# Wide value projections, halved low parts, moved modulation groups and early dilated scores in a two-block transformer kernel

## The chip, the cores and the metric

The kernel runs on one core of a Trainium2 chip, in one launch. The metric is the device time of an execution in microseconds. The engines are TensorE (PE; its weight loads are the row PEld), VectorE (DVE), ScalarE (ACT), GpSimd (POOL) and SyncE (SP), whose queue issues nearly all loads.

## What is computed

256 tokens of width 1024 pass through a first block of two layers, and a second block that is modulated by a conditioning vector `c_2`. The change lies in the second block and in the last attention of the first. In the reference:

```python
mod = jax.nn.silu(c) @ w_ada[l] + b_ada[l]
sh1, sc1, g1, sh2, sc2, g2 = jnp.split(mod, 6, axis=-1)
h = modulate(rms_norm(x, norm1_g[l]), sh1, sc1)
x = x + g1[:, None, :] * token_mixer(h, w_in[l], rel_bias, ...)
h = modulate(rms_norm(x, norm2_g[l]), sh2, sc2)
x = x + g2[:, None, :] * squared_relu_mlp(h, w_ff1[l], w_ff2[l])
```

`token_mixer` projects h with `w_in` into retention queries, keys and values (`rq`, `rk`, `rv`: 4 heads, values 512 wide each), three groups of dilated attention (`aq`, `ak`, `av`: 512 columns each), and gates (`rg`, `ga`, `gb`), runs the retention and the dilated attention, projects both branches, and merges them.

## The kernel before

**Groups and units.** All projections are an ordered list, `PLAN`. A group is one fill of one of three PSUM banks; a unit is one load of at most 128 x 2048 fp32 weights (1 MB). A unit name with "a" or "b" is half of a group's weights. `WEIGHTS`, `LOADS` and the slot tables are worked out from the list: a unit's raw slot is the one whose last unit is oldest, and SP loads it once that unit's group has been read.

**Two precisions.** In the first block the matmuls are plain fp32 (line 571; in the profile each counts as two matmuls). From `rq0` on, a weight unit is split: ScalarE copies its high part to fp32r (`w_hi`, line 1050, called by `passing`), GpSimd subtracts to get the low part (`w_lo`, line 521, one instruction for a unit), and TensorE does three fp32r matmuls for each product: high x high, high x low, low x high (lines 596 to 598, with the weights stationary and 256 tokens moving; lines 628 to 630 for values, with 128 tokens stationary and 256 value columns moving).

**ScalarE's order.** ScalarE works in program order. At each group it comes to, it first calls `passing(name)`:

```python
if max(old, LOADED_AFTER[v]) >= GROUP_AT[name]:
    break
...
act.wait_ge(raw_in[RAW_AT[n]], raw_target(n))
nc.scalar.activation(hi_slots[HI_AT[m]][:, 0:kt * w], raw_slots[RAW_AT[n]][:, 0:kt * w], ACT.Copy)
```

It splits the next units in order, as long as their high slot's last reader and the groups that their load (and all loads ahead of it) waited for come before `name`. `LOADED_AFTER` is the index of the last such group. For rq0 and rq1 it is `ad11`, for rq2 `wo1_1`.

**Modulation.** `mod` is made of 12 groups `ad0` to `ad11`, each of two 1 MB units, 16 matmuls in the profile (line 810), a transpose and a copy on VectorE (lines 1505 and 1507), and is gathered by `modA` and `modB`. They are placed by hand between other work: `FILL_CD` lists, for the 16 units of attention C and D, what is done before and after the transposes of a unit ("/" parts the two). C has 12 units, D 4.

**Attention.** For a unit: scores (TensorE), maximum (VectorE), exponential (ScalarE, line 1116), normalisation (VectorE, line 1484), transposes (TensorE, line 702), copies (ScalarE, line 1134), product with the values. Between C/D and rq0 lies `output(1, ...)`: four groups `wo1_0` to `wo1_3`, residual, squares (ScalarE, line 1098), their sums in pairs (VectorE, line 1683) and over partitions (TensorE, line 644), then the norm of stream x2, whose last steps make `parts`, the split h (line 1383). `output(2, ...)` does the same for x3.

**Block 2's order on TensorE.** rq, rk (8 groups), rv (8 groups of 256 columns), four retention heads with the groups of `RET_FILL` between their steps, the last values av2_0 and av2_1, dilated attention with the gates as fill (`FILL_A`), the branch products `wr0`, `wa0` to `wa3`, `wr1` to `wr3`, the output product `wo2`, then `f1` and `f2`.

## Time and profile before

| | |
|---|---|
| median of 3 runs | 1031.07 us (1030.75 to 1032.62) |
| the profiled execution | 1030.22 us, span 1028.4 us |
| granted TensorE clock, mean | 0.976 |
| busy: PE, PEld, DVE, ACT, POOL | 93%, 85%, 35%, 40%, 43% of the span |
| chain that ended last | PE 84%, DVE 10%, ACT 3%, issue 1%, DMA 1% |

Times in the rows count from the start of the span. A matmul's row gives its latency; back-to-back matmuls overlap, so the distance between starts is what one costs. A number in brackets at a row's end is the idle time of that engine before it, and what ended it. L571 is line 571 of the kernel before.

### The profile page before, as it was taken

To read this page: it belongs to the slowest core of one execution; us is meant where nothing else is said; L and a number is where in the kernel's file an instruction comes from. 1 tells how busy PE (TensorE), PEld (TensorE's weight loads), DVE (VectorE), ACT (ScalarE), POOL (GpSimd) and SP (SyncE) were. 2 spreads that over 40 slices of the span, in tenths; PEclk is the share of its full clock that TensorE was granted. 3 is DMA by queue.
4 is the path that set the end of the run, shared out by engine and by line. 5 is a ranking of instruction groups with operands and counts; after the bars stand their busy time and mean duration, and the time that the engine had idled before them with its cause. 6 is when DMAs were issued, how large, how long until landed. Compare 5 with 4: busy or idle time off the path is not lost.

```text
span 1028.4 us, 15967 instructions
## 1 busy us (share of the span) xinstructions
PE 957.8 (93%) x6896; PEld 874.2 (85%) x6896; DVE 363.5 (35%) x734; ACT 408.1 (40%) x588; POOL 446.0 (43%) x101
## 2 busy tenths in 40 slices
PE   4999889999898798999999998999999979999996
PEld 4887677788676377999999998999999979999996
DVE  4677521320556626640111113222115643341002
ACT  3111541013576423234343444667533545553330
POOL 0000000000000031787766665766787767886780
PEclk9999899999899999999999998999999989999998
DMA  9632245858524363565534443444544625453531
GB/s 353 257 123 82 83 175 205 329 176 316 196 83 164 124 246 126 175 242 183 185 131 158 158 150 111 160 161 152 177 164 164 238 95 200 168 199 130 204 121 41
DMA packets 27470, 177.51 MB, mean 173 GB/s; under 512 B 2904, under 2 KB 5476, under 8 KB 6920
## 3 DMA queue, kind: packets, MB, share of 16 engines
q1 hardware_dynamic: 25960, 174.28, 46.9%
q10 hardware_dynamic: 1440, 2.20, 0.7%
q8 instruction: 55, 0.90, 0.3%
q14 instruction: 15, 0.12, 0.0%
HBM read 174.88 MB, written 3.43 MB: 173 GB/s over the span
## 4 chain that ended last, share of the span: by engine, by line
PE 84%; DVE 10%; ACT 3%; issue 1%; DMA 1%; POOL 0%; DVEq 0%; ACTq 0%
PE proj L571 18%; PE proj L596 14%; PE proj L597 14%; PE proj L598 14%; PE proj L628 3%; PE proj L630 3%; PE proj L629 3%; PE proj L780 3%; PE proj L617 2%; PE transposed L702 2%; PE proj L810 2%; PE mixed L731 1%; PE scores L690 1%; DVE parts L1561 1%; PE scores L677 1%
## 5 line engine op out<-in xcount | busy, mean ns | idle before, releaser
L521 POOL TENSOR_TENSOR w_lo<-raw,w_hi 128x2048 fp32r<-128x2048 f32 x71 | 329.0, 4639 | 269.7 <-ACT w_hi L1050 269.6
L596 PE MATMUL proj<-parts,w_hi 128*128 128x256 f32 x768 | 222.2, 289 | 6.5 <-DVE parts L1383 4.2
L597 PE MATMUL proj<-parts,w_lo 128*128 128x256 f32 x800 | 227.5, 284 | 0.0
L598 PE MATMUL proj<-parts,w_hi 128*128 128x256 f32 x768 | 218.3, 284 | 0.0
L1050 ACT ACTIVATE w_hi<-raw 128x2048 fp32r<-128x2048 f32 x71 | 135.5, 1909 | 99.4 <-PE proj L598 63.8
L596 PEld LDWEIGHTS proj<-parts,w_hi 128*128 128x128 f32 x768 | 148.1, 193 | 8.1 <-issue 5.2
L597 PEld LDWEIGHTS proj<-parts,w_lo 128*128 128x128 f32 x800 | 154.2, 193 | 0.8 <-issue 0.7
L598 PEld LDWEIGHTS proj<-parts,w_hi 128*128 128x128 f32 x768 | 148.0, 193 | 0.0
L525 POOL MEMSET probT<- 128x512 f32 x1 | 0.5, 525 | 247.8 <-PE proj L897 247.8
L571 PE MATMUL proj<-h,raw 128*128 128x256 f32 x320 | 76.5, 403 | 3.0 <-DVE h L1391 3.0
L571 PEld LDWEIGHTS proj<-h,raw 128*128 128x128 f32 x320 | 64.7, 204 | 14.2 <-issue 4.5
L628 PE MATMUL proj<-w_hi,parts 128*128 128x256 f32 x224 | 64.0, 286 | 0.0
L629 PE MATMUL proj<-w_lo,parts 128*128 128x256 f32 x224 | 63.4, 283 | 0.0
L630 PE MATMUL proj<-w_hi,parts 128*128 128x256 f32 x224 | 63.4, 283 | 0.0
L571 PE MATMUL proj<-h,arena 128*128 128x256 f32 x256 | 56.8, 381 | 1.1 <-DVE h L1391 1.1
L571 PEld LDWEIGHTS proj<-h,arena 128*128 128x128 f32 x256 | 48.2, 190 | 10.6 <-issue 3.6
L1098 ACT ACTIVATE wide<-xT 128x512 f32<-128x512 f32 (+1 forms) x24 | 13.2, 556 | 104.8 <-DVE xT L1790 64.0
L571 PE MATMUL proj<-arena 128*128 128x256 f32 x224 | 49.4, 380 | 0.0
L571 PEld LDWEIGHTS proj<-arena 128*128 128x128 f32 x224 | 42.4, 190 | 6.0 <-issue 0.3
L596 PE MATMUL proj<-hid_hi,w_hi 128*128 128x256 f32 x160 | 45.1, 282 | 0.0
L597 PE MATMUL proj<-hid_hi,w_lo 128*128 128x256 f32 x160 | 44.7, 279 | 0.0
L598 PE MATMUL proj<-hid_lo,w_hi 128*128 128x256 f32 x160 | 44.6, 279 | 0.0
(273 smaller groups left out, 1940.5 us busy)
## 6 DMA issues: line engine op xcount, KB each, us to landing
raw<-in_weights SPq DMA_DIRECT2D x113, 1024.0 KB, 4.9
arena<-in_weights SPq DMA_DIRECT2D x36, 1024.0 KB, 5.0
probT<-in_weights SPq DMA_DIRECT2D x8, 1024.0 KB, 5.7
dil_lines<-dil_line SPq DMA_DIRECT2D x1, 2304.0 KB, 12.1
dil_bias<-dil_lines SPq DMA_DIRECT2D x1, 1536.0 KB, 9.6
xT<-in_x SPq DMA_DIRECT2D x2, 512.0 KB, 5.6
arena<-in_alibi SPq DMA_DIRECT2D x1, 1024.0 KB, 20.6
arena<-in_swa SPq DMA_DIRECT2D x1, 1024.0 KB, 7.3
```

Of the source, the lines that this page charges most:

```text
L521: nc.gpsimd.tensor_tensor(lo_slots[RAW_AT[n]][:, 0:kt * w], raw_slots[RAW_AT[n]][:, 0:kt * w], hi_slots[HI_AT[m]][:, 0:kt * w].bitcast(F32 ...
L571: last = nc.tensor.matmul(b[:, S * j:S * j + S], w[:, k, P * j:P * j + P], src[:, k, :], start=first, stop=done and (k == ks[-1] if not wa ...
L596: nc.tensor.matmul(dst, whi, h, start=first, stop=False)
L597: nc.tensor.matmul(dst, wlo, h, start=False, stop=False)
L598: last = nc.tensor.matmul(dst, whi, lo[:, k, :], start=False, stop=stop)
L617: last = nc.tensor.matmul(b[:, S * t:S * t + n], h32[:, k, P * t:P * t + P], w[:, k, 0:n], start=k == 0, stop=k == KD - 1)
L628: nc.tensor.matmul(dst, parts[:, 0, k, at], whi[:, k, c:c + n], start=k == 0, stop=False)
L629: nc.tensor.matmul(dst, parts[:, 0, k, at], wlo[:, k, c:c + n], start=False, stop=False)
L630: last = nc.tensor.matmul(dst, parts[:, 1, k, at], whi[:, k, c:c + n], start=False, stop=k == KD - 1)
L702: last = nc.tensor.transpose(pt[0:w, P * i:P * i + P], prob(u)[:, i, P * r:P * r + w], ident[:])
L780: last = nc.tensor.matmul(b[:, 2 * c:2 * c + S], w[:, k, c:c + P], h32[:, k, :], start=k == 0, stop=k == KD - 1)
L1050: nc.scalar.activation(hi_slots[HI_AT[m]][:, 0:kt * w], raw_slots[RAW_AT[n]][:, 0:kt * w], ACT.Copy) \
```

## The change

- The 14 value groups of 256 columns become seven of 512 columns, each of two units of 512 rows x 512 columns and two PSUM banks, one for each 128 tokens (`token_rows` takes the place of `tokens`). The unit "a" is used for both banks before "b".
- GpSimd makes each low part in two instructions, and TensorE waits for the first half at a unit's start and for the second at its middle (`second_half`).
- `ad8`, `ad9` and `ad11` leave `FILL_CD`, and `ad7` moves by one unit. `ad8` and `ad9` are done before and after the last sum of x2, `ad10` and `ad11` before and after the last sum of x3, with a gathering `modC` of their own after `f1_2`. Their loads move: ad8 and ad9 stand ahead of rq2, ad10 and ad11 ahead of f1_2; from ad9 on they have slots of their own in memory free by then.
- The scores of the first unit of dilated attention are issued ahead of the last value group, those of the second between its halves.
- The slot tables and `LOADED_AFTER` follow from the list. For rq0 and rq1 it is now `ad6`, for rq2 and rq3 `wo1_2`, for f1_2 `wo2_0` as before.

```diff
-RET_FILL = [f"a{n}{g}_{i}" for g in range(AG) for n in "qk" for i in range(2)] + \
-    [f"av{g}_{i}" for g in range(AG) for i in range(2)]
+RET_FILL = [x for g in range(AG) for x in ([f"aq{g}_{i}" for i in range(2)], [f"ak{g}_{i}" for i in range(2)])] + \
+    [[f"av{g}"] for g in range(AG)]
...
-    "/ zd1.1", "/ E:zd1 ad6", "/ modA", "/ ad7", "/ ad8", "/ ad9", "/", "/ ad11")]
+    "/ zd1.1", "/ E:zd1 ad6", "/ modA", "/", "/ ad7", "/", "/", "/")]
...
-    out += own([f"wo1_{i}" for i in range(4)]) + [(n, parts_of(n)) for n in ("ad10",)]
+    out += own([f"wo1_{i}" for i in range(4)]) + [(n, parts_of(n)) for n in ("ad8", "ad9")]
     out += own(["rq0"]) + [("modB", [])]
-    out += own([f"rq{i}" for i in range(1, 4)] + [f"rk{i}" for i in range(4)] + [f"rv{i}" for i in range(8)])
+    rows = lambda n: [(n, [f"{n}a"]), (f"{n}:0", [f"{n}b"]), (f"{n}:1", [f"{n}b"])]
+    dilated = lambda names: rows(*names) if names[0][1] == "v" else own(names)
+    out += own([f"rq{i}" for i in range(1, 4)] + [f"rk{i}" for i in range(4)]) + [x for i in range(RH) for x in rows(f"rv{i}")]
     for h in range(RH):
-        out += own(RET_FILL[4 * h:4 * h + 4]) + [(f"rt{h}_0", []), (f"rt{h}_1", [])]
-    out += own(RET_FILL[16:]) + own(GATED)
+        out += dilated(RET_FILL[2 * h]) + dilated(RET_FILL[2 * h + 1]) + [(f"rt{h}_0", []), (f"rt{h}_1", [])]
+    out += dilated(RET_FILL[8]) + own(GATED)
     out += [(n, [f"{n}a", f"{n}b"] if n[1] == "r" else [f"wa{int(n[2]) // 2}"]) for n in BRANCHES]
-    out += own([f"wo2_{i}" for i in range(4)] + [f"f1_{i}" for i in range(16)])
+    out += own([f"wo2_{i}" for i in range(4)]) + [(n, parts_of(n)) for n in ("ad10", "ad11")]
+    out += own([f"f1_{i}" for i in range(3)]) + [("modC", [])] + own([f"f1_{i}" for i in range(3, 16)])
...
-SPLIT = WEIGHTS[WEIGHT_AT["rq0"]:]
+BANKED = [g for g in GROUPS if f"{g}:1" not in GROUP_AT]
+BANK_AT = {n: i for i, n in enumerate(BANKED)}
+SPLIT = [u for u in WEIGHTS[WEIGHT_AT["rq0"]:] if u[:2] != "ad"]
...
-LOADS = [u for u in WEIGHTS if u[:4] != "ad10"]
-for _n, _u in enumerate(("ad10a", "ad10b")):
-    LOADS.insert(LOADS.index("rq2") + _n, _u)
+LOADS = [u for u in WEIGHTS if u[:3] not in ("ad8", "ad9", "ad1") or u[:4] in ("ad1a", "ad1b")]
+for _before, _us in (("rq2", ("ad8a", "ad8b", "ad9a", "ad9b")), ("f1_2", ("ad10a", "ad10b", "ad11a", "ad11b"))):
+    for _n, _u in enumerate(_us):
+        LOADS.insert(LOADS.index(_before), _u)
...
+        elif u in ALONE:
+            most = max(most, GROUP_AT["wr3" if u[2] == "1" else "ad7"])
...
+                elif u[:3] == "ad9":
+                    sp.wait_ge(po_free, STEPS_TO["d"])
+                elif u[:3] == "ad1":
+                    sp.wait_ge(proj_ready, GROUP_AT["wr3"] + 1)
...
-                nc.gpsimd.tensor_tensor(lo_slots[RAW_AT[n]][:, 0:kt * w], raw_slots[RAW_AT[n]][:, 0:kt * w],
-                                        hi_slots[HI_AT[m]][:, 0:kt * w].bitcast(F32), ALU.subtract).then_inc(lo_ready, 1)
+                for half in range(2):
+                    at = slice(kt * w // 2 * half, kt * w // 2 * (half + 1))
+                    nc.gpsimd.tensor_tensor(lo_slots[RAW_AT[n]][:, at], raw_slots[RAW_AT[n]][:, at],
+                                            hi_slots[HI_AT[m]][:, at].bitcast(F32), ALU.subtract).then_inc(lo_ready, 1)
...
+            def second_half(u, k):
+                if k == unit_shape(u)[0] // 2 and state["lo"] < SPLIT_AT[u]:
+                    pe.wait_ge(lo_ready, 2 * SPLIT_AT[u] + 2)
+                    state["lo"] = SPLIT_AT[u]
...
-            def tokens(name, c, n):
-                b = begin(name)
-                whi, wlo = weight(UNITS_OF[name][0])
-                for t in range(TT):
-                    for k in range(KD):
-                        dst, at = b[:, S * t:S * t + n], slice(P * t, P * t + P)
-                        nc.tensor.matmul(dst, parts[:, 0, k, at], whi[:, k, c:c + n], start=k == 0, stop=False)
-                        nc.tensor.matmul(dst, parts[:, 0, k, at], wlo[:, k, c:c + n], start=False, stop=False)
-                        last = nc.tensor.matmul(dst, parts[:, 1, k, at], whi[:, k, c:c + n], start=False, stop=k == KD - 1)
-                end(last)
+            def token_rows(name, middle=None):
+                banks = [None] * TT
+                for half in "ab":
+                    u = f"{name}{half}"
+                    whi, wlo = weight(u)
+                    for t in range(TT):
+                        if half == "a":
+                            banks[t] = begin(f"{name}:{t}")[:]
+                        for k in range(4):
+                            at, kk = slice(P * t, P * t + P), 4 * (half == "b") + k
+                            nc.tensor.matmul(banks[t], parts[:, 0, kk, at], whi[:, k, :], start=kk == 0, stop=False)
+                            second_half(u, k)
+                            nc.tensor.matmul(banks[t], parts[:, 0, kk, at], wlo[:, k, :], start=False, stop=False)
+                            last = nc.tensor.matmul(banks[t], parts[:, 1, kk, at], whi[:, k, :], start=False, stop=kk == KD - 1)
+                        if half == "b":
+                            end(last)
+                    if half == "a":
+                        last.then_inc(proj_ready, 1)
+                        if middle is not None:
+                            middle()
...
-            output(1, "x2", product, lambda i: ada("ad10") if i == 0 else None)
+            output(1, "x2", product, lambda i: ada(f"ad{8 + i}"))
             project("rq0", fresh=2)
-            pe.wait_ge(sem("ada_cols"), ADA_GROUPS)
-            mod_columns("modB", ADA_ONE, ADA)
+            pe.wait_ge(sem("ada_cols"), ADA_GROUPS - 2)
+            mod_columns("modB", fold, ada_cols, ADA_ONE, ADA_TWO)
             for name in [f"rq{i}" for i in range(1, 4)] + [f"rk{i}" for i in range(4)]:
                 project(name)
-            for i in range(8):
-                tokens(f"rv{i}", 0, 256)
-            def dilated_fill(name):
-                if name[1] == "v":
-                    tokens(name, 0, 256)
-                else:
-                    project(name)
+            for i in range(RH):
+                token_rows(f"rv{i}")
...
-            for name in RET_FILL[16:]:
-                dilated_fill(name)
-            pe.wait_ge(*evacuated("av2_1"))
-            attention(PART["a"], FILL_A)
+            for n in "qk":
+                for i in range(2):
+                    pe.wait_ge(*evacuated(f"a{n}2_{i}"))
+            scores(PART["a"][0])
+            token_rows("av2", lambda: scores(PART["a"][1]))
+            for t in range(TT):
+                pe.wait_ge(*evacuated(f"av2:{t}"))
+            attention(PART["a"], FILL_A, 2)
...
+            pe.wait_ge(sem("late_silu_ready"), 1)
+            output(2, "x3", merged_product, lambda i: ada(f"ad{10 + i}", late_silu))
             for i in range(16):
                 project(f"f1_{i}", fresh=3 if i == 0 else None)
+                if i == 2:
+                    pe.wait_ge(sem("late_fold_in"), 16)
+                    pe.wait_ge(sem("ada_cols"), ADA_GROUPS)
+                    mod_columns("modC", late_fold, late_cols, 0, ADA - ADA_TWO)
...
-            for name in RET_FILL[16:]:
-                dilated_out(name)
-            attention(PART["a"], FILL_A)
+            passing("av2")
+            exps(PART["a"][0])
+            dilated_out(RET_FILL[8])
+            attention(PART["a"], FILL_A, 1)
...
-            ada_out("ad10")
-            mod_out("modB", ADA_ONE, ADA)
+            ada_out("ad8")
+            ada_out("ad9")
+            mod_out("modB", ADA_ONE, ADA_TWO)
+            V.tensor_copy(late_silu, silu_c).then_inc(sem("late_silu_ready"), 1)
...
+            for name in ("ad10", "ad11"):
+                ada_out(name, late_flip, late_cols, 10)
             for i in range(16):
+                if i == 3:
+                    mod_out("modC", ADA_TWO, ADA)
```

## Rows read from the trace of the kernel before

**Rows 1.** The page, busy time in us, share of the span, instructions.
```profile
PE 957.8 (93%) x6896; PEld 874.2 (85%) x6896; DVE 363.5 (35%) x734; ACT 408.1 (40%) x588; POOL 446.0 (43%) x101
```
**Rows 2.** Timeline of ScalarE in the value projections: start us, us.
```profile
485.78 0.60 ACT L1066 ACTIVATE arena<-proj 128x512 f32<-128x512 f32 x1 [3.37 <-PE proj L630]
...
491.54 0.60 ACT L1066 ACTIVATE arena<-proj 128x512 f32<-128x512 f32 x1 [3.37 <-PE proj L630]
```
**Rows 3.** The chain, plain fp32 of 256 and of 512 columns.
```profile
380.00 6.91 PE proj L571 x32
...
510.93 1.72 PE mixed L984 x4
```
**Rows 4.** The page's costliest groups: GpSimd's low parts, one of three value lines.
```profile
L521 POOL TENSOR_TENSOR w_lo<-raw,w_hi 128x2048 fp32r<-128x2048 f32 x71 | 329.0, 4639 | 269.7 <-ACT w_hi L1050 269.6
...
L628 PE MATMUL proj<-w_hi,parts 128*128 128x256 f32 x224 | 64.0, 286 | 0.0
```
**Rows 5.** The chain in attention C/D (L810 is group ad6).
```profile
323.15 1.85 PE proj L810 x16
...
329.59 1.28 ACT L1116
...
332.68 1.11 PE transposed L702 x4
...
339.44 0.64 DVE dil_bias L1505
...
340.10 0.18 DVE arena L1507
```
**Rows 6.** Timeline of SP: loads of rq0 and rq1; the one issued behind wo1_2.
```profile
360.92 0.90 SPq L478 DMA_DIRECT2D raw<-in_weights  x2
...
386.94 0.33 SPq L478 DMA_DIRECT2D arena<-in_weights  x1
```
**Rows 7.** Timeline of ScalarE: splits of rq0 and rq1, x2's last squares.
```profile
367.99 1.91 ACT L1050 ACTIVATE w_hi<-raw 128x2048 fp32r<-128x2048 f32 x1 [4.18 <-DMA raw<-in_weights]
370.40 1.92 ACT L1050 ACTIVATE w_hi<-raw 128x2048 fp32r<-128x2048 f32 x1 [0.50 <-DMA raw<-in_weights]
...
395.01 0.63 ACT L1098 ACTIVATE wide<-xT 128x512 f32<-128x512 f32 x1 [6.68 <-DVE xT L1689]
```
**Rows 8.** Timeline of TensorE: a sum of x2, and behind both norms of block 2.
```profile
379.30 0.70 PE L644 MATMUL sums<-wide,cols 128*128 128x256 f32 x2 [1.85 <-DVE wide L1683]
...
401.74 0.55 PE L596 MATMUL proj<-parts,w_hi 128*128 128x256 f32 x1 [4.15 <-DVE parts L1383]
...
832.66 0.55 PE L596 MATMUL proj<-parts,w_hi_b 128*128 128x256 f32 x1 [4.62 <-DVE parts L1383]
```
**Rows 9.** The chain, a load of 1 MB from issue to landing.
```profile
750.22 4.90 DMA raw<-in_weights
```
**Rows 10.** Timeline of VectorE: three subtractions beside GpSimd's low parts.
```profile
786.96 15.12 DVE L1561 TENSOR_TENSOR parts<-arena,parts 128x512 fp32r<-128x512 f32 x3
```
**Rows 11.** Timeline of TensorE at the start of the dilated attention.
```profile
620.66 0.94 PE L677 MATMUL scores<-arena 128*128 128x128 f32 x6 [0.69 <-ACT arena L1066]
622.63 2.38 PE L677 MATMUL scores<-arena 128*128 128x256 f32 x6 [1.03 <-DVE stat L1426]
626.22 1.65 PE L677 MATMUL scores<-arena 128*128 128x128 f32 x6 [1.21 <-DVE stat L1426]
...
628.10 0.41 PE L598 MATMUL proj<-parts,w_hi 128*128 128x256 f32 x1
628.31 0.41 PE L596 MATMUL proj<-parts,w_hi 128*128 128x256 f32 x1
```
**Rows 12.** Timeline of TensorE ahead of wr3 and inside wo2_0.
```profile
786.64 0.35 PE L596 MATMUL proj<-yret_hi,w_hi_a 128*128 128x256 f32 x1 [2.03 <-POOL w_lo_a L521]
...
804.93 0.38 PE L596 MATMUL proj<-parts,w_hi 128*128 128x256 f32 x1 [1.00 <-DVE parts L1561]
```
**Rows 13.** Busy us in a window (PE, PEld, DVE, ACT, POOL), granted clock, DMA, GB/s.
```profile
786.60:792.00 5.40, 5.36 (x32) 5.39 (x33) 5.40 (x3) 2.55 (x2) 5.26 (x2) 0.68 0.84 350
```

More of the change, by code:

```diff
@@ L139 @@
 EARLY = [NRAW + 2 + i for i in range(3)]
+ALONE = {u: NRAW + 5 + i for i, u in enumerate(("ad9a", "ad9b", "ad10a", "ad10b", "ad11a", "ad11b"))}
 def raw_slots_of(n, u):
+    if u in ALONE:
+        return [ALONE[u]]
     if u in SPLIT_AT:
@@ L531, in _ @@
         def _(pe):
-            state = dict(filled=0, norm=0, head=0, stream=0)
+            state = dict(filled=0, norm=0, head=0, stream=0, lo=-1)
             def begin(name):
-                m = GROUP_AT[name]
+                m = BANK_AT[name]
                 assert state["filled"] <= m < state["filled"] + NPP, name
@@ L782, in chunk, with attention @@
                     end(last)
-            def attention(units, fill):
-                scores(units[0])
-                scores(units[1])
+            def attention(units, fill, begun=0):
+                for u in units[begun:2]:
+                    scores(u)
                 for i, u in enumerate(units):
@@ L986, in _ @@
                     last.then_inc(sem("ret_out"), 1)
-                for i in range(2, 4):
-                    dilated_fill(RET_FILL[4 * h + i])
+                dilated_fill(RET_FILL[2 * h + 1])
                 pe.wait_ge(sem("ret_normed"), 2 * h + 2)
@@ L1027, in _ @@
             stream_sums("xf", 3)
-            assert state["filled"] == len(GROUPS) and state["norm"] == len(NORMS)
+            assert state["filled"] == len(BANKED) and state["norm"] == len(NORMS)
         @block.scalar
@@ L1171, in between, with attention @@
                     copy_out(name, fl((gaT if name[1] == "a" else gbT)[:, 2 * i:2 * i + 2]), fn=ACT.Sigmoid)
-            def attention(units, fill):
-                exps(units[0])
+            def attention(units, fill, begun=0):
+                for u in units[begun:1]:
+                    exps(u)
                 for i, u in enumerate(units):
@@ L1292, in _, with dilated_out @@
                 passing(name)
[L1293 to L1303 removed]
+            for i in range(RH):
+                passing(f"rv{i}")
+                for t in range(TT):
+                    copy_out(f"rv{i}:{t}", rv[:, t, RDV * i:RDV * i + RDV])
+            def dilated_out(names):
+                for name in names:
+                    g, i = int(name[2]), int(name[-1])
+                    if name[1] == "v":
+                        passing(name)
+                        for t in range(TT):
+                            copy_out(f"{name}:{t}", av[:, g, t, :])
+                    else:
+                        copy_out(name, (aqT if name[1] == "q" else akT)[:, g, 512 * i:512 * i + 512],
+                                 scale=P ** -0.5 if name[1] == "q" else 1.0)
             for h in range(RH):
[L1306 to L1308 removed]
+                dilated_out(RET_FILL[2 * h])
+                passing(RET_FILL[2 * h + 1][0])
                 for t in range(TT):
@@ L1311, in _ @@
                     nc.scalar.activation(bn[:, t, 8:9], bn[:, t, 8:9], ACT.Sqrt).then_inc(sem("ret_sqrt"), 1)
-                for i in range(2, 4):
-                    dilated_out(RET_FILL[4 * h + i])
+                dilated_out(RET_FILL[2 * h + 1])
                 for half in range(2):
@@ L1500, in mixed_out, with ada_out @@
                 V.tensor_tensor(y, cut(po[:, 0:S], P), y, ALU.mult).then_inc(po_free, 1)
-            def ada_out(name):
-                g = int(name[2:])
-                V.transpose(ada_flip, ready(name)[:]).then_inc(free_of(name), 1)
+            def ada_out(name, flip=ada_flip, table=ada_cols, first=0):
+                g = int(name[2:]) - first
+                V.transpose(flip, ready(name)[:]).then_inc(free_of(name), 1)
                 dve.wait_ge(*evacuated(name))
-                V.tensor_copy(ada_cols[:, 16 * g:16 * g + 16], cut(ada_flip, HROW)[:, :, 0]).then_inc(sem("ada_cols"), 1)
+                V.tensor_copy(table[:, 16 * g:16 * g + 16], cut(flip, HROW)[:, :, 0]).then_inc(sem("ada_cols"), 1)
                 state["cols"] = state.get("cols", 0) + 1
```

70 lines of the change are left out of this document (36 added, 34 removed).

## The prediction

> **What bounds the kernel now.** I read the page first: TensorE is busy 93% of the span [rows 1], and the chain of work that ended last runs through it for 84%. So work taken off TensorE counts, and work of another engine counts only where TensorE waits for it. Next the timelines of the stages that the diff touches, and the chain of waits, to find those places. They are few: the attention of branches C and D (up to 363 us), where the chain passes from engine to engine [rows 5]; the two norms of block 2, where TensorE stands still for 4.15 and 4.62 us [rows 8]; the start of the dilated attention [rows 11]; and two waits around the last branch product [rows 12]. Everything from rq0 to av2 is back to back.
>
> **Value projections (removes 672 fp32r matmuls of 256 columns, adds 336 of 512).** One group of 48 old matmuls takes 5.76 us, the distance of the copies behind two groups [rows 2]: 120 ns each. There are 14 such groups, 224 matmuls in each of three lines [rows 4]. No fp32r matmul of 512 columns is in the trace. If the time went with the columns it would be 240 ns: gain nothing. The other end is the plain pass, in which 256 columns take 6.91/32 = 216 ns and 512 take 1.72/4 = 430 ns [rows 3], 214 for 256 more: almost no fixed part. At full clock 256 columns of fp32r need half a plain pass, 108 ns, and take 120, so 12 ns is something else: hidden when the matmul is longer (216 ns for 512), or paid once per matmul (228 ns). At half clock the pitch is 0.21 us [rows 11], exactly twice 107, with no 12 ns on top, which speaks for hiding. I take 220: 336 x (240 - 220) = -6.7 us, bounds 0 and -8.1.
> The Trainium skill (TensorE: Matmul & The Clock Gate, "Back-to-back issue gap") gives columns/2.4 + 2.5 ns: 216 ns for 512, by which the gain would be 8.1 us. By that rule 256 columns would take 109 ns, and the trace shows 120, so it is not followed to the end here.
>
> **First dilated scores around the last values.** Before, TensorE ends av2_1 at 619.97, waits 0.69 for the copy, does the scores of three units with waits of 1.03 and 1.21 between them, and starts rg0 at about 627.5, at half clock [rows 11]: 7.6 us. After, unit 0's scores lie before av2, unit 1's between its halves, where VectorE has 5 us to take the banks. What stays is three units at full clock, 6 x 0.108 + 6 x 0.216 + 6 x 0.108 = 2.6 us, and one copy wait, 0.7: 3.3 us. That is -4.3. The twelve matmuls of rg0 at 213 instead of 120 ns cost 1.1, and go too: -5.4 (bounds -3 and -6).
>
> **Low parts in halves.** A low part is 4.64 us of GpSimd [rows 4]. Two halves are 2.3 us each if time goes with size; a shorter one is not in the trace. A fixed cost matters only above 0.27 us a half, since TensorE needs 24 x 216 = 5.2 us for a unit. TensorE can start on the first half. Where weights are ready early this gains nothing, which is nearly everywhere. It gains before wr3: TensorE waits 2.03 us, until 786.6, for a low part that must have begun at about 782.0 [rows 4, 12]; its first half is done at 784.3, before TensorE is free at 784.6. Behind that wait the granted clock is 0.68 for 5.4 us [rows 13], that is some 3.4 us at half rate, 1.7 us lost. Together -3.7. But VectorE's subtractions stand behind GpSimd: three of them took 15.12 us [rows 10], one behind each GpSimd instruction. With halves each waits at most 2.3, yet the last subtraction before wo2_0 still comes two halves, a scale and a copy after wr3, so the wait of 1.00 [rows 12] grows by about 1.2. Net -2.5 (bounds -3.7 and -1).
> The Trainium skill (SBUF — State Buffer, "Who interferes with whom") says a VectorE instruction with two SBUF inputs and a GpSimd one that reads SBUF exclude each other for a whole instruction. The trace agrees [rows 10]. It also means that two such VectorE instructions in a row gain nothing from halves: the second waits for the second half. I count none for the rotary.
>
> **Modulation groups moved.** A group is 1.85 us of TensorE, and 0.64 of VectorE for the transpose and 0.18 for the copy [rows 5]. Three leave C/D. TensorE waits there for VectorE, so what counts is two times 0.85 of VectorE on the chain (at 339.44, and once more at 351.87) and most of the 1.85 of ad11: -3.3. The groups that arrive later lie in the two norm waits [rows 8]; ad10 of block 2's second norm stands in front of the last sum and costs some 0.5 us.
>
> **What moves with them: loads, and ScalarE's splits.** This is the part that speaks against the change. ScalarE works in order, and its routine passing() splits every unit whose slots are free by the group it stands at, waiting for the load. Removing ad8, ad9 and ad11 from the list frees rq0's and rq1's raw slots early: they count as loaded after ad6, not ad11. So ScalarE does them at modA, ahead of the exponentials of unit 11. Their loads are third and fourth of four that SP issues when ad6 has been read, at 325.0 (1.85 us from 323.15) [rows 5]. A lone megabyte lands 4.90 us after its issue [rows 9]; in a line they land 2.4 us apart (splits at 367.99 and 370.40 for loads of 360.92) [rows 6, 7]. So rq0 lands at 325.0 + 4.9 + 2 x 2.4 = 334.7, rq1 at 337.1; with 1.91 us for a split, ScalarE is free at 339.0. Before, it went on at 329.59, and from there to TensorE's transposes at 332.68 the chain runs through it [rows 5]. Cost +9.5 us, all of it on the chain. Behind it GpSimd's two low parts run into VectorE's normalisation of unit 11: +0.8 (0 to 2.3).
> For the same reason the splits of rq0 and rq1 are gone from the output stage, and with them the low part that held VectorE's sum of squares and TensorE for 1.85 us [rows 8]: -1.85.
> rq2 moves too. Before, it was loaded ahead of ad10b; now SP issues it fourth behind ad8b, ad9a and ad9b, when wo1_2 has been read at 386.9 [rows 6]. It lands at 386.9 + 4.9 + 3 x 2.4 = 399.0. ScalarE must split it at wo1_3, before the last squares, which began at 395.01 [rows 7]. So the squares end at 399.0 + 1.9 + 0.6 = 401.5, TensorE's four sums at 402.6 instead of 397.6 (401.74 less the 4.15 us) [rows 8]. +5.0, and +0.5 as rq2's low part holds the norm's first product: +5.5 (bounds 4 and 7).
> In the second norm f1_2 is behind four modulation loads in the same way, but about 22 us after wr3 it still lands almost in time: +0.7 with ad10.
>
> **The clock.** C/D has less TensorE work and one pause of 10 us; the first norm's pause is longer too; in the second, ad11 shortens a pause of 4.62 us. A stretch at half clock of 3.4 us costs 1.7. I take +1.0 (bounds -2 and +6).
>
> **The sum:** -6.7 -5.4 -2.5 -3.3 -1.85 +9.5 +0.8 +5.5 +0.7 +1.0 = -2.3 us. I leave half a microsecond for waits of VectorE behind the second half of a low part (two ada_out in a row ahead of modB among them): -1.8. The profiled execution took 1030.22 us (span 1028.4 and 1.8 around it), so 1028.4; the median of the runs is 0.85 above it: 1029.3 us.
>
> **Rivals.** (1) *ScalarE's waits are cheap*: the loads land earlier than in my line, or the exponentials behind them had slack. For it: the chain near 330 changes engines every microsecond. Against it: both splits are fixed by the order on ScalarE, and 3.8 us of them is pure work. Without both waits (-9.5 - 0.8 - 5.5): 1013.5 us; with half of them 1021. (2) *The wide matmuls gain nothing*: the fp32r pass is bound by 0.469 ns a column. For it: 120 ns for 256 columns and no wide fp32r row. Against it: the half-clock pitch [rows 11]. It gives +6.7, 1036 us, and decides (slower than before) from a pitch above 228 ns on, all else as summed. (3) *The clock*: C/D and the first output product run at half rate, which adds 5 us: 1034.5. For it: the removed groups were what filled TensorE there, and a pause of 2.03 us was enough to lower the clock before wr3 [rows 12, 13]. Against it: behind the pauses of 1.85 and 1.00 us it stayed up [rows 8, 12].
>
> **Chances.** Forecast 0.50 (own range 1024 to 1034), rival 1 0.14, rival 2 0.16, rival 3 0.20. A measurement of this kernel can tell about 0.2%, 2.1 us. The forecast gives 0.30 faster, 0.15 same, 0.05 slower; rival 1 is all faster; rival 2 gives 0.13 slower, 0.03 same; rival 3 0.12 slower, 0.05 same, 0.03 faster. Together 0.47, 0.23, 0.30. The range is 1017 to 1037: below it lies rival 1 in full, above it rivals 2 and 3 together.
>
> **What the profile after would show.** The wide matmuls' pitch between two value copies (220 ns or 240); a ScalarE idle of 5 us ended by a load at about 330, with TensorE still until about 342; a split of rq2 ended by a load at about 399 less the shifts before, with the last squares behind it; the dilated scores split around av2 with one wait; no wait before wr3. It is wrong above all if ScalarE does not stand still at modA, or if the exponentials of unit 11 were not what the chain needed.

## The result, and the profile after

The changed kernel takes 1037.19 us in the median of 11 runs (1036.38 to 1040.58), the kernel before 1031.09 in 11 runs beside it (1029.12 to 1036.76). The ratio is 1.0054, 95% interval 1.0035 to 1.0072: slower by 5.6 us, where 1029.3 was forecast; it lies just above the range. The profiled execution took 1039.65 us, its span is 1037.9, 9.5 more than before.

The page of the kernel after: the span, busy time by engine, the chain by engine, and GpSimd's low parts.

```profile
span 1037.9 us, 15403 instructions
...
PE 958.2 (92%) x6562; PEld 855.9 (82%) x6562; DVE 394.5 (38%) x739; ACT 409.2 (39%) x588; POOL 467.6 (45%) x197
...
PE 83%; DVE 9%; DMA 4%; ACT 2%; issue 1%; SPq 0%; DVEq 0%; ACTq 0%
...
L542 POOL TENSOR_TENSOR w_lo<-raw,w_hi 128x1024 fp32r<-128x1024 f32 x142 | 341.3, 2426 | 271.6 <-ACT w_hi L1096 271.6
```

What has grown is DMA, from 1% to 4% of the chain: TensorE ends up waiting for loads, through ScalarE. To see where, I set the same instruction of both traces side by side. The shift is its start after less its start before; the last columns are what each stretch added and what the prediction's terms say for it.

| up to | before | after | shift | added | forecast |
|---|---|---|---|---|---|
| transposes ahead of modA | 327.23 | 328.66 | 1.4 | +1.4 | 0 |
| transposes behind the splits (C/D) | 332.68 | 344.48 | 11.8 | +10.4 | +9.5 |
| last product of D | 362.34 | 374.81 | 12.5 | +0.7 | -1.5 |
| third x2 sum | 394.08 | 406.82 | 12.7 | +0.3 | -1.85 |
| rq0 | 401.74 | 421.95 | 20.2 | +7.5 | +5.5 |
| scores of retention head 1 (holds rv) | 524.87 | 541.52 | 16.65 | -3.6 | -3.8 |
| products of head 3 (holds av0) | 593.27 | 609.32 | 16.05 | -0.6 | -1.0 |
| wr0 (holds av1, av2, the early scores) | 738.95 | 748.47 | 9.5 | -6.5 | -7.3 |
| wo2_0 | 804.93 | 811.52 | 6.6 | -2.9 | -2.5 |
| third x3 sum | 818.94 | 824.99 | 6.05 | -0.5 | 0 |
| f1_0 | 832.66 | 842.63 | 10.0 | +3.9 | +0.7 |
| last f2 sums | 1018.37 | 1027.84 | 9.5 | -0.5 | 0 |

(A value group's share of -6.7 is one in seven, 0.96: four in the line of head 1, whose measured -3.6 holds 1.1 us of another cause, rq0 at full clock. The row of D holds three terms: -3.3 for the groups removed, +1.0 for the clock, +0.8 for the low parts behind the splits. The half microsecond held back for waits of VectorE is in no row.) The change wins nearly what it should from rq1 to wo2_0 and loses it at three places. Here they are in the timelines of the kernel after (start, duration, engine, line, operation, tiles, count, and in brackets the idle time before it with what ended it).

C/D, first ScalarE, then TensorE:

```profile
330.41 0.59 ACT L1180 ACTIVATE probT<-transposed 128x512 f32<-128x512 f32 x1
337.00 1.91 ACT L1096 ACTIVATE w_hi<-raw 128x2048 fp32r<-128x2048 f32 x1 [6.00 <-DMA raw<-in_weights]
339.45 1.91 ACT L1096 ACTIVATE w_hi<-raw 128x2048 fp32r<-128x2048 f32 x1 [0.54 <-DMA raw<-in_weights]
341.38 1.28 ACT L1162 ACT_TABLE_LOAD   x1
...
331.61 0.33 PE L856 MATMUL proj<-arena 128*128 128x64 f32 x2
344.48 1.11 PE L741 MATMUL transposed<-cols,wide 128*128 128x128 f32 x4 [12.53 <-ACT probT L1180]
...
348.57 1.03 PE L741 MATMUL transposed<-cols,prob 128*15 128x128 f32 x4 [0.97 <-DVE prob L1535]
...
354.24 3.64 PE L849 MATMUL proj<-raw,arena 128*32 128x512 f32 x16
```

ScalarE stands 6.54 us for the loads of rq0 and rq1 and works 3.82 us on them, together 10.36: the 10.4 that the stretch added. Behind it ad7 takes 3.64 us instead of the 1.92 of a group at full clock: half clock. The low parts of rq0 and rq1 run on GpSimd from 338.99 to 348.24, and VectorE beside them:

```profile
343.97 1.99 DVE L1524 TENSOR_SCALAR stat<-stat 128x4 f32<-128x4 f32 x1 [10.49 <-ACT prob L1162]
...
346.21 2.05 DVE L1533 TENSOR_TENSOR stat<-stat,arena 128x4 f32<-128x4 f32 x1
```

With the splits out of the way (late splits, below) these two take 0.17 and 0.16 us. TensorE waits 0.97 us for their result at 348.57: that is the +0.8 of the forecast.

The x2 output, with SP's issues, ScalarE and TensorE:

```profile
399.68 0.80 SPq L496 DMA_DIRECT2D arena<-in_weights  x2
...
401.00 1.41 SPq L496 DMA_DIRECT2D raw<-in_weights  x2
...
413.25 1.91 ACT L1096 ACTIVATE w_hi<-raw 128x2048 fp32r<-128x2048 f32 x1 [12.21 <-DMA raw<-in_weights]
415.06 0.61 ACT L1144 ACTIVATE wide<-xT 128x512 f32<-128x512 f32 x1
...
407.35 1.92 PE L849 MATMUL proj<-arena 128*32 128x512 f32 x16
415.73 2.07 PE L683 MATMUL sums<-wide,cols 128*128 128x256 f32 x4 [6.46 <-ACT wide L1144]
417.73 3.41 PE L849 MATMUL proj<-arena 128*32 128x512 f32 x16
421.95 0.35 PE L623 MATMUL proj<-parts,w_hi 128*128 128x256 f32 x1 [0.81 <-DVE parts L1434]
```

The first of the line's loads is issued at 399.68, rq2 as the fourth at 401.00. ScalarE's split of rq2 starts at 413.25, 12.25 us behind its own issue and 13.6 behind the line's first; ScalarE has stood for it 12.21 us with the last squares behind it.

The x3 output, in the same order and with VectorE's fold:

```profile
806.29 2.28 SPq L496 DMA_DIRECT2D arena<-in_weights  x4
813.24 18.44 SPq L496 DMA_DIRECT2D raw<-in_weights  x4
...
828.52 1.92 ACT L1096 ACTIVATE w_hi<-raw 128x2048 fp32r<-128x2048 f32 x1 [7.97 <-DMA raw<-in_weights]
830.34 0.61 ACT L1144 ACTIVATE wide<-xT 128x512 f32<-128x512 f32 x1
...
830.99 2.18 DVE L1734 TENSOR_TENSOR wide<-wide 128x256 f32<-128x256 f32 x1 [4.93 <-ACT wide L1144]
...
833.22 0.70 PE L683 MATMUL sums<-wide,cols 128*128 128x256 f32 x2 [1.90 <-DVE wide L1734]
833.85 3.56 PE L849 MATMUL proj<-arena,sq 128*32 128x512 f32 x16
842.63 0.36 PE L623 MATMUL proj<-parts,w_hi_b 128*128 128x256 f32 x1 [2.30 <-DVE parts L1434]
```

The same once more, and not foreseen: f1_2's load, issued at 813.24 behind seven megabytes (wo2_3, f1_0, f1_1 and the four of ad10 and ad11, from 804.97 on), lands for a split at 828.52. Squares, fold and sum are late in turn, and ad10 runs at half clock.

The wide matmuls, by ScalarE's copies of the token half 0 of two value units:

```profile
478.57 0.60 ACT L1108 ACTIVATE arena<-proj 128x512 f32<-128x512 f32 x1 [0.80 <-PE proj L664]
...
489.45 0.60 ACT L1108 ACTIVATE arena<-proj 128x512 f32<-128x512 f32 x1 [0.80 <-PE proj L664]
```

10.88 us for 48 matmuls: 227 ns each, against 2 x 120 before [rows 2].

### The profile page after: what moved, and what is told of

Its sections match the earlier page's. It is cut to its first block, busy times and chain, and to the rows that moved or that the text cites. A ratio compares the mean times of both kernels' runs of the same rounds, so it can differ in the third digit from the quotient of the medians.

```text
span 1037.9 us, 15403 instructions
## 1 busy us (share of the span) xinstructions
PE 958.2 (92%) x6562; PEld 855.9 (82%) x6562; DVE 394.5 (38%) x739; ACT 409.2 (39%) x588; POOL 467.6 (45%) x197
## 4 chain that ended last, share of the span: by engine, by line
PE 83%; DVE 9%; DMA 4%; ACT 2%; issue 1%; SPq 0%; DVEq 0%; ACTq 0%
PE proj L598 17%; PE proj L623 14%; PE proj L626 14%; PE proj L625 14%; DMA raw<-in_weights 4%; PE proj L819 3%; PE proj L664 2%; PE proj L663 2%; PE proj L661 2%; PE proj L645 2%; PE proj L849 2%; PE transposed L741 2%; PE mixed L770 1%; PE scores L729 1%; DVE rstd L1438 1%
## 5 line engine op out<-in xcount | busy, mean ns | idle before, releaser
L542 POOL TENSOR_TENSOR w_lo<-raw,w_hi 128x1024 fp32r<-128x1024 f32 x142 | 341.3, 2426 | 271.6 <-ACT w_hi L1096 271.6
L598 PEld LDWEIGHTS proj<-h,raw 128*128 128x128 f32 x320 | 63.3, 199 | 13.7 <-issue 4.5
L1108 ACT ACTIVATE arena<-proj 128x512 f32<-128x512 f32 x40 | 23.9, 598 | 78.0 <-PE proj L626 48.8
L661 PE MATMUL proj<-w_hi,parts 128*128 128x512 f32 x112 | 44.4, 396 | 0.0
L1860 DVE TENSOR_TENSOR hid_lo<-tmp,hid_hi 128x512 fp32r<-128x512 f32 x16 | 43.7, 2732 | 0.6
## 6 DMA issues: line engine op xcount, KB each, us to landing
dil_lines<-dil_line SPq DMA_DIRECT2D x1, 2304.0 KB, 12.1
```

The lines of the kernel that those rows point to most:

```text
L542: nc.gpsimd.tensor_tensor(lo_slots[RAW_AT[n]][:, at], raw_slots[RAW_AT[n]][:, at], hi_slots[HI_AT[m]][:, at].bitcast(F32), ALU.subtract).t ...
L598: last = nc.tensor.matmul(b[:, S * j:S * j + S], w[:, k, P * j:P * j + P], src[:, k, :], start=first, stop=done and (k == ks[-1] if not wa ...
L661: nc.tensor.matmul(banks[t], parts[:, 0, kk, at], whi[:, k, :], start=kk == 0, stop=False)
L1108: nc.scalar.activation(dst, b[:], fn, scale=scale).then_inc(free_of(name), 1)
L1860: V.tensor_tensor(two(hid_lo, i), r, two(hid_hi, i).bitcast(F32), ALU.subtract).then_inc(sem("hid_ready"), 1)
```

## Experiments

Times are turned into microseconds as ratio x 1032; "less than after" compares the ratio of a kernel with 1.0054. The times of one kernel spread: those of the kernel before, all visits together, from 1026.9 to 1038.1 us. Some of it is the granted clock in the attention of D, which differs between two executions of one kernel ("Two profiles of one kernel"). So small differences are checked in traces.

### Mending the orders: three places

**Late splits.** In ScalarE's passing():

```diff
+                    if v in ("rq0", "rq1"):
+                        old = GROUP_AT["ad7"]
```

> The kernel after, but ScalarE splits rq0 and rq1 only from wo1_0 on, when the attention of branches C and D is over; the loads and everything else stay. Main theory (ScalarE standing still 6.0 us for rq0's load and working 3.8 us on the two splits is what moved TensorE's transposes from 332.68 to 344.48 us, and the half clock behind it is the consequence of that pause): TensorE's pause is gone, the clock in D is full, and the time falls by 8 to 11 us, to about 1028 us; up to 2 us of it are given back since GpSimd's low parts of rq0 or rq1 meet VectorE's squares of the x2 sum again. Rival (the pauses in D and its half clock come from the three modulation groups that no longer fill TensorE there): the clock stays at half in D and only the 4 us of pure waiting go: 1033 us or more. If ScalarE had slack there: no change, 1037 us.

**rq2 first.** In the list of loads:

```diff
-for _before, _us in (("rq2", ("ad8a", "ad8b", "ad9a", "ad9b")), ...
+for _before, _us in (("rq3", ("ad8a", "ad8b", "ad9a", "ad9b")), ...
```

> The kernel after, but rq2 is loaded ahead of ad8a, ad8b, ad9a and ad9b (right behind wo1_3), so that ScalarE needs not wait for it before the last squares of the x2 sum. Main theory (TensorE's 6.46 us at the last x2 sum are the wait of ScalarE for rq2, fourth in its line of loads): the wait falls to about 1 us, the sums and ad9 run at full clock, and the time falls by 5 to 8 us, to about 1031 us. Rival (the wait goes to the next in the line: ad9, now loaded last, is what TensorE waits for behind the sums): 0 to 2 us, 1036 us.

**Both.**

> Both edits at once: rq0 and rq1 split from wo1_0 on, and rq2 loaded ahead of ad8 and ad9. Main theory: the two losses are independent and add up: 13 to 17 us less than the kernel after, about 1022 us, well under the kernel before. Rival (they share a cause, or the early load only moves the low parts of GpSimd in front of VectorE's squares): not more than the better of the two alone, 1028 us.

Late splits: ratio 0.9935 (0.9912 to 0.9957), 12.3 us less than after. rq2 first: 1.0002 (0.9985 to 1.0020), 5.4 less. Both: 0.9883 (0.9862 to 0.9904), 17.7 less, which is the sum of the two. rq2 first lies in its expected range of 5 to 8 us; late splits, expected at 8 to 11, and both, expected at 13 to 17, won a little more than their ranges. The main theory holds for all three, and the kernel with both is well under the one before. In the trace of the kernel with late splits, TensorE's pause and its successors read so:

```profile
334.35 0.66 PE L741 MATMUL transposed<-cols,wide 128*128 128x128 f32 x4 [2.17 <-ACT probT L1182]
...
364.12 1.97 PE L770 MATMUL mixed<-probT,arena 128*64 128x128 f32 x16 [0.69 <-ACT probT L1182]
...
405.36 2.07 PE L683 MATMUL sums<-wide,cols 128*128 128x256 f32 x4 [6.43 <-ACT wide L1146]
```

12.53 us of waiting have become 2.17, while the 6.43 at the x2 sum stand as they were: they are the other place's. One expectation failed: the clock in D is not full again. The lines give, from the transposes behind the splits to the last product of D, the length, TensorE's busy time and, third from the end, the granted clock, for the kernel before (the profile of the prediction), after, late splits, and the kernel before profiled again:

```profile
332.68:362.34 29.66, 21.55 (x192) 11.57 (x192) 19.18 (x50) 12.15 (x45) 0.00 (x0) 0.94 0.32 112
```
```profile
344.48:374.81 30.33, 20.12 (x145) 12.24 (x145) 20.15 (x46) 12.29 (x45) 3.76 (x2) 0.73 0.00 1
```
```profile
334.35:364.12 29.77, 20.55 (x144) 12.48 (x144) 16.52 (x44) 12.39 (x45) 0.00 (x0) 0.64 0.13 56
```
```profile
332.89:367.92 35.03, 26.56 (x193) 13.48 (x193) 19.17 (x50) 12.16 (x45) 0.00 (x0) 0.76 0.28 98
```

0.73 with the pause ahead, 0.64 without it, over the same instructions. So the half clock in D does not need the pause. The rival's clock came true, but not its time. Its cause, the three groups gone, is not shown: with the groups in place the second profile of the kernel before has 0.76.

**Three orders.** The x3 output mended too: f1_2 loaded ahead of ad10, f1_3 ahead of ad11.

```diff
-... ("f1_2", ("ad10a", "ad10b", "ad11a", "ad11b"))):
+... ("f1_3", ("ad10a", "ad10b")), ("f1_4", ("ad11a", "ad11b"))):
```

> The kernel with both orders mended (1020.3 us), and in the x3 output f1_2 loaded ahead of ad10a and ad10b, f1_3 ahead of ad11a and ad11b. There, ScalarE stood 8.11 us for f1_2's load with the squares of the third sum behind its split, and TensorE stood 2.03 us and then ran at half clock. Main theory (a third case of a weight load placed behind modulation loads): that idle time of ScalarE and the 2.03 us go, ad10 takes 1.9 us instead of 3.4, and the time falls by 3 to 4 us, to about 1017 us. Rival (TensorE now waits for ad11's load, or the gain lies within the norm's own wait): 0 to 1 us.

Ratio 0.9838 (0.9812 to 0.9864), 4.6 us less than with two orders (0.9862 to 0.9904; the intervals just touch). TensorE there:

```profile
813.13 0.59 PE L683 MATMUL sums<-wide,cols 128*128 128x256 f32 x2
813.65 1.92 PE L849 MATMUL proj<-arena,sq 128*32 128x512 f32 x16
815.50 1.13 PE L683 MATMUL sums<-wide,cols 128*128 128x256 f32 x4
816.56 1.92 PE L849 MATMUL proj<-arena,sq 128*32 128x512 f32 x16
821.27 0.35 PE L623 MATMUL proj<-parts,w_hi_b 128*128 128x256 f32 x1 [2.78 <-DVE parts L1436]
```

No wait before the third sum, and both groups at full clock inside what was the norm's pause: this is what the move of the groups was meant to look like.

**Held splits.** The other cure: no load is moved, only ScalarE's order, at all three places.

```diff
+                    held = {"rq0": "ad7", "rq1": "ad7", "rq2": "ad9", "f1_2": "ad11", "f1_3": "ad11"}.get(v)
+                    if held is not None:
+                        old = max(old, GROUP_AT[held])
```

> The kernel after with every load where it is, and only ScalarE's order changed at all three places: rq0 and rq1 are split from wo1_0 on, rq2 from rq0 on, f1_2 and f1_3 from f1_0 on, behind the squares that they held. If the harm is ScalarE waiting in order, and not the place of the loads as such: as good as the three mended orders of loads, about 1016 us. Rival (the low parts then fall on VectorE's products of the norms, which TensorE waits for): 1019 to 1024 us.

Ratio 0.9833 (0.9816 to 0.9851), 1015.43 us: as good as the three orders and the lowest median here, 1.7% under the kernel before. So what did the harm is ScalarE waiting in order ahead of work that the chain needs; the late loads alone cost nothing that can be measured here. The rival's collision is there and small: TensorE waits 0.90 us at modB and 1.45 at rq2 for VectorE.

**Early loads.** The loads of rq0 and rq1 put ahead of wo1_0, as soon as their slots are read.

```diff
+for _u in ("rq0", "rq1"):
+    LOADS.remove(_u)
+    LOADS.insert(LOADS.index("wo1_0"), _u)
 LOADS.remove("wo1_3")
-LOADS.insert(LOADS.index("rq1") + 1, "wo1_3")
+LOADS.insert(LOADS.index("wo1_2") + 1, "wo1_3")
```

> The kernel after, but rq0 and rq1 are loaded ahead of wo1_0 (as soon as their slots come free, behind zc1 and zd0), so that ScalarE splits them earlier in C and never waits for their data. It tells the two parts of the loss apart. Main theory (the waiting for the loads, some 6.5 us, is the larger part, and two splits of 1.91 us with GpSimd's low parts beside VectorE the smaller): 5 to 8 us less than the kernel after, about 1031 us. If the work alone is the trouble (ScalarE's chain is that tight, and a low part holds VectorE wherever it falls): 0 to 3 us less, 1035 us.

A miss: 1.0049 (1.0032 to 1.0065), nothing gained. ScalarE in C, then TensorE:

```profile
300.73 1.91 ACT L1099 ACTIVATE w_hi<-raw 128x2048 fp32r<-128x2048 f32 x1 [3.31 <-DMA raw<-in_weights]
...
320.06 1.91 ACT L1099 ACTIVATE w_hi<-raw 128x2048 fp32r<-128x2048 f32 x1 [1.95 <-DMA raw<-in_weights]
```
```profile
308.16 1.11 PE L744 MATMUL transposed<-cols,prob 128*128 128x128 f32 x4 [4.85 <-DVE prob L1538]
...
327.03 0.61 PE L744 MATMUL transposed<-cols,prob 128*15 128x128 f32 x4 [2.91 <-DVE prob L1538]
...
343.45 0.66 PE L744 MATMUL transposed<-cols,wide 128*128 128x128 f32 x4 [2.17 <-ACT probT L1183]
```

The splits moved forward with the loads, because passing() takes each unit as soon as the group that read its slot is behind: the load is issued at that same moment. ScalarE still waits 5.26 us, and TensorE's pauses stand in C instead (in the trace of late splits it does not wait there). I had thought the waiting would be gone; it went from 6.54 to 5.26 only, so this run doesn't tell waiting from work. That the loss is both (6.54 + 3.82) rests on the trace of after alone.

### The parts one by one

**Groups back.** All of the change but the move of the modulation groups: FILL_CD, the list of loads, the x2 and x3 outputs and modB as before.

> The kernel after with the modulation groups where they were before (ad8, ad9 and ad11 in C and D, ad10 at the x2 output, none in the x3 output), all else as after: wide value projections, low parts in halves, early dilated scores. Main theory (only the move of the groups loses time; the after trace shows 227 ns for a wide matmul, so 4.5 us won, 5.5 for the early scores, 2.9 before wo2_0): 1031.1 - 12.9 = 1018 us. Rival (halves of low parts cost VectorE and GpSimd time elsewhere, or the wide matmuls win nothing): 1024 to 1031 us.

Ratio 0.9864 (0.9833 to 0.9896), 14.0 us under the kernel before. The three other parts were forecast at -6.7 - 5.4 - 2.5 = -14.6. So the move, as it was made, costs 5.6 + 14.0 = 19.6 us. From here each of the three is taken out again.

**Values 256 wide.** The same loops and banks, two matmuls of 256 columns for each of 512:

```diff
-nc.tensor.matmul(banks[t], parts[:, 0, kk, at], whi[:, k, :], ...)
+for c in (slice(0, 256), slice(256, 512)):
+    nc.tensor.matmul(banks[t][:, c], parts[:, 0, kk, at], whi[:, k, c], ...)
```

> The kernel with the modulation groups back (1018.5 us), but each matmul of 512 columns of the value projections is made as two of 256, in the same loops, units and banks: the width alone. From the pitch of 227 ns in the trace against twice 120: 336 x 13 ns = 4.4 us more, about 1023 us. If the width were worth nothing: no change. If the wide matmul took 216 ns it would have been 8 us.

0.9891 (0.9870 to 0.9912), 2.8 us more; medians 1022.66 against 1018.54, 4.1. The intervals overlap, and the traces give the size: from the last product of D to the first dilated scores that stand behind av2 this kernel takes 625.50 - 366.14 = 259.4 us, groups back 621.95 - 366.78 = 255.2: 4.2.

**Whole low parts.** GpSimd makes a low part in one instruction:

```diff
-for half in range(2):
-    at = slice(kt * w // 2 * half, kt * w // 2 * (half + 1))
-    nc.gpsimd.tensor_tensor(lo_slots..., ...).then_inc(lo_ready, 1)
+nc.gpsimd.tensor_tensor(lo_slots..., ...).then_inc(lo_ready, 2)
```

> The kernel with the modulation groups back (1018.5 us), but GpSimd makes each low part in one instruction again. By the shift between the traces of before and after from wr0 to wo2_0 the halves won 2.9 us: 1021.5 us, with TensorE waiting some 2 us ahead of wr3 again. If they cost as much in VectorE's waits elsewhere as they win: no change.

0.9932 (0.9905 to 0.9960), 7.0 us more, twice what was expected, and the wait of some 2 us ahead of wr3 did not come: TensorE waits 0.56 us there and 2.90 at wo2_0. The kernel before, profiled again (last section of the experiments), has the same two waits, where its first profile had 2.03 and 1.00 [rows 12]:

```profile
791.46 0.35 PE L596 MATMUL proj<-yret_hi,w_hi_a 128*128 128x256 f32 x1 [0.56 <-POOL w_lo_a L521]
...
810.14 0.39 PE L596 MATMUL proj<-parts,w_hi 128*128 128x256 f32 x1 [2.93 <-DVE parts L1561]
```

VectorE at the end of f1, and TensorE in f2's first group, which began at 919.39:

```profile
923.12 5.00 DVE L1833 TENSOR_TENSOR hid_lo<-tmp,hid_hi 128x512 fp32r<-128x512 f32 x1
928.04 5.04 DVE L1831 TENSOR_TENSOR tmp<-tmp 128x512 f32<-128x512 f32 x1
```
```profile
933.86 0.39 PE L607 MATMUL proj<-hid_hi,w_hi 128*128 128x256 f32 x1 [3.70 <-DVE hid_lo L1833]
```

From wr0 to wo2_0 the halves win 2.0 us between these two traces, and f2 begins 0.7 us later with whole low parts. Most of the loss is behind that: with whole low parts VectorE's instruction takes 5.00 us beside one of GpSimd, TensorE stands 3.70 us in f2's first group for the last part of its input, and the granted clock is 0.85 over the 11.1 us behind the pause, against 1.00 for groups back. With halves VectorE's instruction takes 2.89 us and there is no wait. The kernel before has none in either of its profiles, with whole low parts too. Why it comes in the one and not in the other is open.

**Late scores.** The first dilated scores behind av2 again.

> The kernel with the modulation groups back (1018.5 us), but the scores of the first three dilated units stand behind av2 again. By the traces the early scores won 5 to 5.5 us: 1024 us, with waits of TensorE for ScalarE and VectorE of 0.7, 1.0 and 1.2 us between them and half clock behind.

0.9882 (0.9859 to 0.9904), 1.9 us more; medians 3.7. From the last product of D to the first product of branch A's last mixing: 367.5 against 364.6, 2.9 us. The waits of 0.73, 1.03 and 1.22 are back as expected:

```profile
620.53 0.91 PE L701 MATMUL scores<-arena 128*128 128x128 f32 x6 [0.73 <-issue]
622.46 1.56 PE L701 MATMUL scores<-arena 128*128 128x256 f32 x6 [1.03 <-DVE stat L1454]
625.24 0.94 PE L701 MATMUL scores<-arena 128*128 128x128 f32 x6 [1.22 <-DVE stat L1454]
```

but the six matmuls of the second unit take 1.56 us, at full clock, where both profiles of the kernel before have them at half (2.38, and scores of the third unit 1.65 [rows 11]). The early scores win 2.9 us between these two traces; that they win some 2 more where the clock would have been low is an estimate from the 5.2 between the traces of before and after.

### Two profiles of one kernel

> The kernel before, unchanged, for a second profile of it. In the profile that the prediction was worked out from, the attention of D, from the transposes at 332.68 to the last product at 362.34, takes 29.7 us, mostly at full clock; in four profiles of kernels with the same instructions there it takes 35.0, partly at half clock. If that is chance, this one may show 35 us as well, and if there is something in the kernel before that keeps the clock up, it shows 29.7 again.

> The kernel with the modulation groups back, unchanged, for a second profile and more times. Its six times fell in two groups, 1014.5 to 1015.5 and 1021.6 to 1022.8 us, and its profile (1021.7) shows D at half clock in part, 35.0 us from the transposes to the last product. If the two groups are the granted clock in the attention of D, a profile of about 1015 us shows some 29.7 us there (as the first profile of the kernel before did), and one of about 1022 us shows 35.0 again. If the groups come from elsewhere, the stage is 35.0 us in both.

The kernel before again took 1036.38 us, 6.2 more than in its first profile. Its TensorE, from the transposes to the last product of D:

```profile
332.89 1.12 PE L702 MATMUL transposed<-cols,wide 128*128 128x128 f32 x4 [2.17 <-ACT probT L1134]
...
367.92 1.10 PE L731 MATMUL mixed<-probT,arena 128*64 128x128 f32 x16 [0.69 <-ACT probT L1134]
```

35.0 us for the instructions that took 29.7 in the first [rows 5]: 5.4 of the 6.2 us, at a granted clock of 0.76 instead of 0.94 (the windows above). Groups back gave 35.0 again, in an execution of 1019.61 us; over both visits its times are 1014.5 to 1015.5 (four) and 1019.6 to 1022.8 (six). No profile fell into the quick group, so that it is the clock in D there too is likely and not shown.

## Why the prediction was wrong

**Right, with their sizes.** The stall of ScalarE in C/D: +9.5 forecast, 10.4 measured, made of the idle time and the two splits that were named, and shown by the late splits; the collision with the low parts, +0.8, is a wait of 0.97. The early scores: -5.4 forecast; about -5.2 between the traces of before and after (6.5 less two value units), 2.9 where the clock is full anyway. With the values and the halves -14.6 was forecast, and groups back measures -14.0; the whole agrees better than its parts, which cost 2.8 (values), 7.0 (halves) and 1.9 us (scores) by ratio when they are taken out one at a time.

**The halves** came out near their size in part by luck. Between the traces of before and after they win 2.9 us up to wo2_0 (-2.5 forecast), no wait before wr3 is left, and the wait at wo2_0 has grown from 1.00 to 2.26 us, as the working had it. But the 2.03 us before wr3 and the low clock behind them (0.68 [rows 13]), on which the term was built, are those of one execution. In the second profile of the kernel before the wait is 0.56 us, the granted clock behind it 1.00, and the wait at wo2_0 2.93; the stretch from wr0 to wo2_0 takes 64.95 us instead of 65.98. Against that, and against whole low parts in groups back, the halves win 1.9 to 2.0 us, and they shorten the wait at wo2_0 (2.90 to 2.16) where the working had them lengthen it. That they also guard f2's first group was not seen.

**The wide matmuls**: the mechanism held, the term was mis-sized. 227 ns instead of 220, so 336 x 13 = -4.4 us for -6.7, on the "paid once per matmul" bound that I had given (228). The half-clock pitch, twice 107 ns, had made me lean to hiding; it doesn't carry over to full clock. The turning point of rival 2 was also worked out wrong: a forecast of -1.8 us is used up at 220 + 1.8/0.336 = 225 ns, not at 228, so by the prediction's own sum the measured pitch takes the gain away. The Trainium skill (TensorE: Matmul & The Clock Gate, "Back-to-back issue gap") would give 216 ns by its formula for an isolated matmul, and the trace has 227, as it had 120 where the formula has 109: both are 11 ns above it.

**The second norm** is the step that failed outright: "about 22 us after wr3 it still lands almost in time: +0.7". I counted f1_2 behind four modulation loads, but wo2_3, f1_0 and f1_1 stand ahead of those, all issued within 4 us: from 804.97, 4.90 for the first and seven times 2.46 make 827, and the split came at 828.52. And I looked at when TensorE needs f1_2, not at when ScalarE reaches its split, which is ahead of the third squares. +3.9 us in the trace, 4.6 in the run that mends it (three orders), where 0.7 was forecast.

**The first norm** has the right cause with two terms missing. ScalarE had rq2 13.7 us after wo1_2 had been read (399.5), where the sum had 12.1 (4.9 + 3 x 2.4): it was issued only 1.5 us after that, behind three others, and came 12.25 us after its own issue. And behind the pause the four sums ran at half clock, 2.07 us for 1.13: 5.0 + 1.5 + 0.9 = 7.4, and 7.5 was added. The half clock that rival 3 had at this place came with the pause: with rq2 first, without it, the same sums take 1.13 us.

**The clock in C/D** was the third miss, and here the basis of a term failed, the -3.3 for ad8, ad9 and ad11 leaving C/D. In the seven profiles without them, the stretch from the transposes to the last product takes 29.8 to 30.3 us; in six of seven with them 35.0, and in one 29.7: the one that I read. Against that one the removal wins nothing (+0.7), against the others 5.2. The clock takes part of what the removal gives: ad7, now in the place of ad8, runs at half clock (3.64 us) in all seven profiles without the groups, where ad8 took 1.92 us in the profile that I read and 3.0 to 3.2 in the other six. Likewise wo1_0, partly at half clock: its first 31 matmuls take 8.48 us for 6.96 before, 1.5 of the 1.85 us that the vanished stall of the x2 sum gave.

Of the rivals, the first (ScalarE's waits cheap) is refuted by the late splits, 12.3 us. The second (the wide matmuls gain nothing) is refuted: 4.2 to 4.5 us. The third had the right sign and place, half clock in D and at the x2 output, but it was not decisive: an estimate of some 3 to 5 us of the 11.8 by which the sum was off. From -2.3 forecast to +9.5 between the two profiles the misses are: second norm 3.2, values 2.3, C/D behind the splits 2.2, x2 sum 2.2, first norm 2.0, start 1.4 (by execution: the same transposes start at 325.7 to 328.9 in the profiles of kernels that don't differ up to there), the splits in C/D 0.9, 14.2 in all, less 2.4 that rq0 (now at full clock), wo2 and f2 gave back without a term.

**Was the move worth anything?** With its orders mended the kernel has a ratio of 0.9838 or 0.9833; without the move it has 0.9864 and, on the second visit, 0.9880 (0.9833 to 0.9926). That points to 3 to 5 us won, with overlapping intervals, so it is not shown. And it hangs on the spread: the four quick executions of groups back, 1014.5 to 1015.5 us, are as fast as held splits (1015.2 to 1015.9), and only its six others are slower. Held splits has no slow one in its five, and the stretch of D takes 29.8 to 30.3 us in all seven profiles without the groups. As made the move cost 19.6. The best version, held splits, beats the kernel before by 17 us and the changed one by 23.

## What to carry to other kernels

When a transfer is moved, go through every queue behind it, and ask of each engine that works in order not when its consumer needs the data, but when the engine reaches the instruction that waits, and what stands behind that: here one cause bit at three places, and 23 us lay in the order of five splits. Count everything in the line of loads, from its last pause on, not only what was moved. And before a term rests on a stretch that changes engines every microsecond, profile the same kernel twice: in D 5.4 us hung on the execution, and a wait of 2.03 us before wr3 was 0.56 in the next one.

## What the runs showed of the hardware

- The same instructions of the same kernel (D, from its transposes to its last product) took 29.66 us at a granted clock of 0.94 in one execution and 35.03 us at 0.76 in another; over its second part, from the products behind ad8 on, it was 1.00 against 0.75 (18.3 and 22.6 us).
- A pause of 12.5 us ahead of D was followed by half clock (0.50) for 13.3 us, but without the pause the same instructions ran at 0.56, and the whole stretch at 0.64 against 0.73.
- An fp32r matmul of 512 columns takes 227 ns back to back at full clock, one of 256 takes 120: 107 ns for 256 columns more, and 13 that are paid once.
- A half low part takes 2.43 us of GpSimd, the whole 4.64 [rows 4], so two halves cost 0.21 us more; VectorE's instruction beside it falls from 5.0 to 2.9 us.
- In a line of 1 MB loads, counted from the issue of the line's first, the third was there after 10.5 us (rq0), the fourth after 13.6 (rq2) and the eighth after 23.5 (f1_2): 2.7 to 2.9 us a place behind the 4.90 of a lone one [rows 9], however late within the line each was issued (f1_2 8.3 us after the first).
